# A hybrid recurrent decoder step on one core: the head of the program in another order

## The reference, cut to what matters

```python
def rmsnorm(x, g):
    y = x * lax.rsqrt(jnp.mean(x * x, axis=-1, keepdims=True) + EPS)
    return y * g
...
h = rmsnorm(x, g_mix[0])
z = h @ w_in_e[0]                       # 2048 -> 6 * 1024
xa, ga, q, fz, v, gb = jnp.split(z, EVEN_SPLIT_IDX, axis=-1)
...
lb = lb_logits ...                      # bound of the decay, per channel
logf = logaddexp(log(max(lb, 1e-30)), log1p(-lb) + log_sigmoid(fz))
k = (1 - lb) * sigmoid(-fz)
a = exp(-8 * sigmoid(r) * softplus(-lam_a))   # decay of the recurrence
...
x = x + mix;  x = x + conv_ffn(x)       # then a second layer, and a last rmsnorm
```

## Time and profile before

| | us |
|---|---|
| median of 3 runs | 2743.65 (2742.02 to 2745.71) |
| the profiled execution | 2744.42 |
| its span | 2742.7 |
| PE busy | 2699.8 (98%) |
| DVE busy | 1586.9 (58%) |
| ACT busy | 1176.5 (43%) |
| mean granted clock of PE | 0.993 |

### The profile page before, as it was taken

How to read it: one execution, slowest core, us unless ns; L and a number is a source line. 1 busy time by engine, 2 the same in 40 slices (tenths; PEclk the granted TensorE clock), 3 DMA queues, 4 the chain that set the end, 5 groups by cost and what they waited for, 6 DMA issues and landing times.

```text
span 2742.7 us, 54189 instructions
## 1 busy us (share of the span) xinstructions
PE 2699.8 (98%) x20003; PEld 2672.7 (97%) x20003; DVE 1586.9 (58%) x2605; ACT 1176.5 (43%) x1518; POOL 446.8 (16%) x533
## 2 busy tenths in 40 slices
PE   7999999999999999999999998999999999999998
PEld 7999999999999999999999996999999999999998
DVE  7556666665554455665556647565554555455554
ACT  5554455434343333435554343544433344333444
POOL 1333333330000000070003571310000000000023
PEclk9999999999999999999999999999999999999999
DMA  6444454555554545445454531555555555555543
GB/s 174 132 134 133 127 147 133 143 144 158 143 141 140 147 140 143 132 139 150 138 143 141 149 97 32 150 145 146 152 145 147 152 147 143 148 157 146 147 139 118
DMA packets 738479, 383.00 MB, mean 140 GB/s; under 512 B 13464, under 2 KB 734660, under 8 KB 738404
## 3 DMA queue, kind: packets, MB, share of 16 engines
q1 hardware_dynamic: 723088, 367.96, 47.1%
q0 software_dynamic: 2560, 7.29, 1.1%
q10 hardware_dynamic: 12756, 6.69, 0.8%
HBM read 373.31 MB, written 8.57 MB: 139 GB/s over the span
## 4 chain that ended last, share of the span: by engine, by line
PE 96%; DVE 3%; ACT 1%; issue 0%; DMA 0%; SPq 0%; DVEq 0%; ACTq 0%
PE banks L1629 31%; PE banks L1630 30%; PE banks L1631 30%; PE banks L1694 1%; PE banks L1909 0%; DMA xin<-in_x_sample 0%; DVE wl L1064 0%; DVE m L1506 0%; DVE m L1504 0%; PE banks L1690 0%; PE banks L2010 0%; PE banks L1792 0%; PE banks L1790 0%; DVE m L1505 0%; PE banks L1923 0%
## 5 line engine op out<-in xcount | busy, mean ns | idle before, releaser
L1064 DVE TENSOR_TENSOR wl<-raw,wh 128x1024 fp32r<-128x1024 f32 x708 | 899.3, 1271 | 802.1 <-ACT wh L496 801.1
L1629 PE MATMUL banks<-h,wh 128*128 128x336 f32 (+2 forms) x3648 | 1155.3, 317 | 3.9 <-DVE wl L1112 2.2
L496 ACT ACTIVATE wh<-raw 128x1024 fp32r<-128x1024 f32 x708 | 748.8, 1058 | 941.5 <-PE banks L1631 925.6
L1630 PE MATMUL banks<-h,wh 128*128 128x336 f32 (+2 forms) x3648 | 1146.2, 314 | 0.0
L1631 PE MATMUL banks<-h,wl 128*128 128x336 f32 (+2 forms) x3648 | 1144.9, 314 | 0.0
L1629 PEld LDWEIGHTS banks<-h,wh 128*128 128x128 f32 x3648 | 686.3, 188 | 11.7 <-issue 7.9
L1630 PEld LDWEIGHTS banks<-h,wh 128*128 128x128 f32 x3648 | 686.2, 188 | 1.7
L1631 PEld LDWEIGHTS banks<-h,wl 128*128 128x128 f32 x3648 | 685.9, 188 | 0.0
L1629 PE MATMUL banks<-act,wh 128*128 128x336 f32 (+2 forms) x1872 | 589.8, 315 | 2.6 <-DVE act L1580 2.0
L1630 PE MATMUL banks<-act,wh 128*128 128x336 f32 (+2 forms) x1872 | 586.5, 313 | 0.0
L1631 PE MATMUL banks<-act,wl 128*128 128x336 f32 (+2 forms) x1872 | 585.9, 313 | 0.0
(11 more groups left out here) (383 smaller groups left out, 1698.3 us busy)
## 6 DMA issues: line engine op xcount, KB each, us to landing
raw<-in_w_up SPq DMA_DIRECT2D x172, 512.0 KB, 4.0
raw<-in_w_gate SPq DMA_DIRECT2D x172, 512.0 KB, 3.9
raw<-in_w_down SPq DMA_DIRECT2D x160, 448.0 KB, 3.7
raw<-in_w_in_e SPq DMA_DIRECT2D x96, 512.0 KB, 3.8
raw<-in_w_out_e SPq DMA_DIRECT2D x32, 512.0 KB, 3.9
raw<-in_w_down SPq DMA_DIRECT2D x32, 512.0 KB, 3.9
raw<-in_w_in_c SPq DMA_DIRECT2D x16, 512.0 KB, 3.9
raw<-in_w_glu_v SPq DMA_DIRECT2D x16, 512.0 KB, 3.9
```

What stands on the lines that cost most here:

```text
L496: sc.activation(wh[:, j % RING, :], raw[:, j % RING, :], ACT.Copy).then_inc(rounded, 1)
L1064: v.tensor_tensor(wl[:, j % RING, :], raw[:, j % RING, :], wh[:, j % RING, :].bitcast(F32), ALU.subtract) \
L1629: pe.matmul(out, whi, hi, start=first and k == 0, stop=False)
L1630: pe.matmul(out, whi, lo, start=False, stop=False)
```

## The change

PE's queue begins with 28 matmuls of ones by ones (128 x 128, fp32) into a bank that nobody reads; the memset of ones is the DVE's first instruction. Then come the gains, chunks 0 to 11, and tile 0, with chunks 12 and 13 turned in its middle and 14 and 15 behind it. Tiles 0 and 1 wait for h_lo chunk by chunk (first_h) rather than once for all.

The transfers are reordered: column quarters 0 and 1, then weight tile 0, then row set 5 (which holds lam_a and lb), then quarters 2 and 3, then tiles 1 to 3 and the other rows. Two of the five parts of quarters 0 and 1 are issued by ACT's queue.

ACT's squares are three instructions of 2048 columns behind the chunk loop instead of twelve of 512 within it, and ACT copies seven of the chunks to X. DVE copies the rest, chunks 11 to 15 after the loop. Tile 0 is rounded and split after chunk 7, tile 1 after chunk 14. The reciprocal and the root are made of the sums (128 x 3) rather than of rs (128 x 336), so that the diagonal by ones gives rs at once, and DVE only copies it. That product (token_factors) and seven of the row sets now stand behind tile 3, and row set 5 behind tile 1. Row sets share banks side by side, so that PE needn't wait for ACT's copies, and ACT makes 3 copies of them instead of 7.

```diff
--- before.py
+++ after.py
+X_BY_ACT = (0, 1, 3, 4, 6, 7, 9)
+SPLIT_AFTER = (7, 14)
...
-        sqj, tsq, tss, DG = union(0, ("sqj", [P, 3, 4, D // 4]), ("tsq", [P, 3, 4]), ("tss", [P, 4]), ("DG", [P, 3, P]))
+        sqj, tsq, DG = union(0, ("sqj", [P, 3, D]), ("tsq", [P, 3]), ("DG", [P, 3, P]))
...
-        XB = (*bank[1:5], bank[6], bank[0])
-        RB = (bank[5], bank[3], bank[4], bank[6])
+        XB = bank[1:7]
+        row_sets = {0: (bank[0], 0, 80), 5: (BO, 0, 88), 1: (bank[4], 0, 86), 2: (bank[4], 86, 86), 3: (bank[5], 0, 86),
+                    4: (bank[5], 86, 86), 6: (bank[6], 0, 64), 7: (bank[6], 64, 96), 8: (bank[6], 160, 96)}
...
         @block.sync
         def _(e):
             e.dma_start(ident[:], a["c_ident"]).then_inc(consts_in, 16)
-            for g in (0, 2, 3):
-                x_columns(e, g)
+            for g in range(2):
+                x_columns(e, g, (2, 1, 3))
...
                 load(ph, 0, j, a["w_in_e"][0], 8 * (j % 2), 8, columns[j // 2])
+                if j == 0:
+                    load_rows(e, 5, head_rows_in)
+                    for g in range(2, 4):
+                        x_columns(e, g, range(5))
                 if j == RING - 1:
                     e.dma_start(masks[:], a["c_masks"]).then_inc(rows_in, 16)
...
+                    for q in (6, 7, 8, 1, 2, 3, 4):
+                        load_rows(e, q, rows_in)
...
-            x_columns(e, 1)
+            x_columns(e, 0, (4, 0))
+            load_rows(e, 0, gains_in)
+            x_columns(e, 1, (4, 0))
...
+            def token_squares(t):
+                n = (P, P, T - 2 * P)[t]
+                sc.activation(sqj[0:n, t, :], xin[0:n, t, :], ACT.Square, accum_out=tsq[0:n, t:t + 1]).then_inc(tok_sq, 1)
+
+            row_columns(1, (0,))
             e.wait_ge(rows_c, 1)
+            for c in range(DC):
+                e.wait_ge(x_t, c + 1)
+                if c in X_BY_ACT:
+                    sc.activation(X[:, c, :], XB[c % 6][:, 0:T], ACT.Copy)
+                sc.activation(h[:, c, 0, :], XB[c % 6][:, 0:T], ACT.Copy, scale=col("g_mix", c)).then_inc(h_hi, 1)
+                if c in SPLIT_AFTER:
+                    round_first(SPLIT_AFTER.index(c))
+            e.wait_ge(used, RING)
+            e.wait_ge(masks_made, 1)
             for g in range(4):
-                for c in range(4 * g, 4 * g + 4):
-                    e.wait_ge(x_t, c + 1)
-                    sc.activation(h[:, c, 0, :], XB[c % 6][:, 0:T], ACT.Copy, scale=col("g_mix", c)).then_inc(h_hi, 1)
-                if g >= 2:
-                    round_first(g - 2)
                 e.wait_ge(x_in[g], 80)
-                for t, n in enumerate((P, P, T - 2 * P)):
-                    ins = sc.activation(sqj[0:n, t, g, :], xin[0:n, t, g * (D // 4):(g + 1) * (D // 4)], ACT.Square,
-                                        accum_out=tsq[0:n, t, g:g + 1])
-                ins.then_inc(tok_sq, 1)
-            e.wait_ge(used, RING)
-            for j in (2, 3):
-                round_first(j)
-            norm_root(0)
-            for q in range(1, 9):
-                row_columns(q)
-            e.wait_ge(rows_c, 9)
+            round_first(2)
+            token_squares(0)
+            round_first(3)
+            token_squares(1)
+            token_squares(2)
+            row_columns(2, (5,))
+            e.wait_ge(ms_inv, 1)
+            sc.activation(tsq[:], tsq[:], ACT.Sqrt).then_inc(rstd, 1)
+            for turned, qs in ((4, (1, 2)), (6, (3, 4)), (9, (6, 7, 8))):
+                row_columns(turned, qs)
             e.wait_ge(lam_v, 1)
...
+            v.memset(ones[:], 1.0).then_inc(ones_made, 1)
             v.memset(tiny[:, 11, 0:1], 0.0).then_inc(split, CREDIT)
...
             for c in range(DC):
                 e.wait_ge(h_hi, c + 1)
-                v.tensor_copy(X[:, c, :], XB[c % 6][:, 0:T])
+                if c < 11 and c not in X_BY_ACT:
+                    keep(c)
...
-                if c in (11, 14):
-                    split_first((c - 11) // 3)
-            e.wait_ge(tok_sq, 4)
-            v.tensor_reduce(tss[:, 0:2], tsq[:, 0:2, :], mybir.AxisListType.X, ALU.add)
-            st.then(v.tensor_reduce(tss[0:80, 2:3], tsq[0:80, 2:3, :], mybir.AxisListType.X, ALU.add))
-            for t, n in enumerate((P, P, T - 2 * P)):
-                ins = v.tensor_scalar(DG[0:n, t, 0:n], ident[0:n, 0:n], tss[0:n, t:t + 1], None, ALU.mult)
-            ins.then_inc(diag_made, 1)
+                if c in SPLIT_AFTER:
+                    split_first(SPLIT_AFTER.index(c))
+            keep(12).then_inc(x_kept, 1)
+            split_first(2)
+            for c in (11, 13, 14, 15):
+                keep(c).then_inc(x_kept, 1)
+            split_first(3)
+            e.wait_ge(tok_sq, 3)
+            st.then(v.tensor_scalar(tsq[:], tsq[:], 1.0 / D, EPS, ALU.mult, ALU.add))
+            v.reciprocal(tsq[:], tsq[:]).then_inc(ms_inv, 1)
...
-            for j in (2, 3):
-                split_first(j)
-            norm_inverse(0)
-
+            e.wait_ge(rstd, 1)
+            for t, n in enumerate((P, P, T - 2 * P)):
+                ins = v.tensor_scalar(DG[0:n, t, 0:n], ident[0:n, 0:n], tsq[0:n, t:t + 1], None, ALU.mult)
+            ins.then_inc(diag_made, 1)
+            e.wait_ge(ms_done, 1)
+            st.then(v.tensor_copy(rs[:], BO[:, 0:T]))
...
-            e.wait_ge(rows_c, 9)
+            e.wait_ge(rows_c, 2)
...
+            e.wait_ge(ones_made, 1)
+            for k in range(28):
+                pe.matmul(BO[:, 0:P], ones[:], ones[:], start=True, stop=True)
+            e.wait_ge(consts_in, 16)
+            e.wait_ge(gains_in, 48)
+            rows_turned(0)
+            for c in range(12):
+                turned(c)
...
+                    if not ended and j == 2:
+                        e.wait_ge(x_kept, 1)
+                    half = None
                     if not ended and j == 0:
-                        e.wait_ge(h_lo, DC - 4)
-                    if not ended and j == 1:
-                        token_mean_squares()
-                        e.wait_ge(h_lo, DC)
-                    half = None
+                        half = lambda: (turned(12), turned(13))
+                    x = from_h if ended or j > 1 else first_h
...
+                    if not ended and j == 0:
+                        turned(14)
+                        turned(15)
                     if not ended and j == 1:
-                        e.wait_ge(rows_in, 16 * 16)
-                        for q in range(1, 9):
-                            if q >= 5:
-                                e.wait_ge(rows_c, q - 3)
+                        e.wait_ge(head_rows_in, 8 * 16)
+                        rows_turned(5)
+                    if not ended and j == 3:
+                        e.wait_ge(x_kept, 5)
+                        token_factors()
+                        e.wait_ge(rows_in, 8 * 16)
+                        for q in (1, 2, 3, 4, 6, 7, 8):
                             rows_turned(q)
```

More of the change, by code:

```diff
@@ L330, in build, with x_columns, load_rows @@
         ]
[L332 removed]
+        def x_columns(eng, g, parts):
             xp, xsm = a["x_prompt"][0], a["x_sample"].rearrange("s t d -> (s t) d")
             cols = slice(g * (D // 4), (g + 1) * (D // 4))
[L336 to L337 removed]
+            rows_of = ((0, 0, META, a["meta_tokens"]), (0, META, P, xp[0:P - META]), (1, 0, P, xp[P - META:2 * P - META]),
+                       (2, 0, META, xp[2 * P - META:SEQ]), (2, META, META + NS * LS, xsm))
+            for t, r0, r1, src in (rows_of[k] for k in parts):
                 eng.dma_start(xin[r0:r1, t, cols], src[:, cols]).then_inc(x_in[g], 16)
+        def load_rows(eng, q, arrived):
+            r = 0
+            for src, n in rowsets[q]:
+                eng.dma_start(rows[r:r + n, q, :], src).then_inc(arrived, 16)
+                r += n
         def one(t, c):
@@ L504, in norm_root, with row_columns @@
                 sc.activation(rs[:], rs[:], ACT.Sqrt).then_inc(rstd, 1)
[L506 to L509, removed]
-            x_columns(e, 1)
[L512 to L516, removed]
+            x_columns(e, 0, (4, 0))
+            load_rows(e, 0, gains_in)
+            x_columns(e, 1, (4, 0))
+            def row_columns(turned, qs):
+                b, n = row_sets[qs[0]][0], sum(row_sets[q][2] for q in qs)
+                c0 = (0, 80, 166, 252, 338, 424, 512, 576, 672)[qs[0]]
+                e.wait_ge(rows_t, turned)
+                sc.activation(prm[:, c0:c0 + n], b[:, 0:n], ACT.Copy).then_inc(rows_c, 1)
             def round_first(j):
@@ L1091, in _ @@
             v.memset(tiny[:, 11, 7:8], 0.0).then_inc(y_c, 2)
-            v.memset(ones[:], 1.0)
             v.memset(AT[:], 0.0)
+            v.memset(tsq[:], 1.0)
             e.wait_ge(consts_in, 16)
@@ L1658, in rows_turned, with turned @@
             def rows_turned(q):
-                w = (80, 86, 86, 86, 86, 88, 64, 96, 96)[q]
```

(8 more changed lines are left out.)

22 lines of the change are left out of this document (12 added, 10 removed).

## The result

| | before | changed |
|---|---|---|
| median of 22 runs each, us | 2743.94 (2741.04 to 2746.75) | 2748.64 (2745.81 to 2751.62) |
| ratio, 95% interval | | 1.0018 (1.0012 to 1.0024) |
| the profiled execution | 2744.42 | 2750.07 |
| its span | 2742.7 | 2748.4 |
| level 0 starts at | 47.19 | 53.04 |

The change costs 4.7 us. The forecast was 2749.8, 1.2 above the median, and + 6.2 at level 0, where + 5.85 was measured. The interval excludes "no change", though the difference lies under the 0.2% (5.5 us) that the prediction took as its bound. All of the profiled difference arises ahead of level 0, in these two executions.

The account below looks back on a forecast made before the run. PE is busy for 96%, but the stage was taken to end with the chain from the turned constants: 41.45 + 4.2 + 7.76 puts level 0 at 53.4, + 6.2 on 2743.65 gives 2749.8 us; range 2743.5 to 2753.5.

Parts of the forecast that it names:

- the chain from the turned constants: Through ACT's copies, DVE, Exp, split of tile 4, FZ and Q to level 0: 34.25 + 12.94 = 47.19 us before.
- Predicted end 10.45: PE's front: 28 products of ones end at 1.2 + 5.9 + 3.35 = 10.45 us; bounds 7.5 and 13.8.
- the sum's 5.9 us: PE's products of ones: dense work at half clock for 5.9 us before the clock rises, 13.1 products slow.
- The 14 copies: Chunk loop up to chunk 7: ACT's 14 copies at 0.42 each, 5.9 us; tile 0 starts at 19.35.
- the prediction's last sentence: Wrong if tile 4 follows at once, level 0 precedes 49, or PE waits for xin or raw in the head.
- just hidden: Quarter 2's last part, issued at about 12, lands by about 18 or 19, ahead of tile 0; at most 1 us otherwise.
- My 1.87 for the issue of tile 0: SP's queue ahead of quarter 2: issuing weight tile 0 takes 7.47 / 4 = 1.87 us, row set 5 some 3.5.
- the rival that had 0.17: It falls once more: clock drops in PE's 2.8 us idle ahead of tile 1; + 8 to + 9.2, 2752; chance 0.17.
- These three terms: Tile 1 at 29.6 to constants at 41.45, 4.2 to the split at 45.65, 7.76 to level 0 at 53.4.
- the side that had 0.46: Outcome "same", a difference within 0.2% (5.5 us): chance 0.46; slower 0.49, faster 0.05.
- The clock stays up: PE rises early in the products and doesn't fall in the loop, tile 0 fast: + 2.1, 2745.8 us; chance 0.22.
- The head start is kept: Tile 4's weights ready when constants are turned: level 0 at 45.9, 1.3 ahead, up to 6.9 us faster; chance 0.08.

Follow-up runs that it names:

- both edits: Changed kernel with row set 5, the Exp and DVE's operations on the constants ahead of tile 1, and seven row sets turned behind tile 1: 1.0006 of before.
- the factors early: On top of both edits: product by ones behind tile 2, rs copied behind the splits of tiles 4 and 5, squares spread: 2740.46 us, 0.9989 of before.
- without products: Changed kernel without the 28 products of ones at its front: 2749.05 us, 1.0017 of before.
- the clock kept up: Changed kernel with further products of ones, 2 behind each of chunks 5 to 10 and 8 behind chunk 11: 2751.12 us, 1.0027 of before.
- the constants early: Changed kernel with row set 5 turned ahead of tile 0, its copy, the Exp and DVE's operations on the constants behind chunk 11: 2746.28 us, 1.0006 of before.
- all three with the factors early: The kernel with the factors early with 28, 12 or no products of ones: 0.9989, 0.9989 and 0.9986 of before.
- the two single edits: Changed kernel with only the seven row sets turned behind tile 1 (1.0014 of before), or only the constants' operations early (1.0006).

## Why the prediction was right

**Where the time goes.** The prediction's central step was that the stage ends with the chain from the turned constants, and that the change moves its start. The chain in the trace is that one. The run with both edits, in which two of its entrances are open, and the one with the factors early, in which it is gone, show it as the cause: level 0 went from 53.04 to 49.90 to 45.13, and the ratio from 1.0018 to 1.0006 to 0.9989. From level 0 to the end the profiled executions of all kernels took 2693.2 to 2698.1, without order, so nothing of the loss is seen to come later, within this scatter of 5 us.

**The products.** Predicted end 10.45, gains turned at 10.37. They take 0.43 us each and then 0.22, where the prediction had 0.45 and 0.225 from the product by ones in the earlier trace rows, and which of the two from the transposes. The Trainium skill, "TensorE: Matmul & The Clock Gate", Part 1 on the clock gate, has the clock throttled by default and released by activity: the rate agrees, the column of the granted clock (1.00 from the start) doesn't. But the moment of the rise isn't fixed. Over the eight profiled executions with 28 products it came 3.4 to 5.9 us after the first of them, and they ended between 9.15 and 10.4; the changed kernel's is the latest of the eight. That the sum's 5.9 us and 10.45 were met so closely is luck.

**The chunk loop and quarter 2.** The 14 copies took from 11.00 to 16.51, so 0.39 each where I had 0.42, and tile 0 started at 19.03, not 19.35. Quarter 2 did bind PE's transposes of chunks 8 to 11, for 1.78 us. By the prediction's last sentence a wait of PE for xin is a sign that it is wrong, so on this point it was. As a cover for tile 0, which it had called just hidden, it held: ACT rounded tile 0 from 16.51 on while PE turned these chunks, and tile 0 came no later. The chain of waits leads through this transfer all the same (9.79 to 15.67, then the transposes and 1.92 of "issue"), so the cover was nearly used up. My 1.87 for the issue of tile 0 was wrong; I had divided a group by its count, and row set 5 took 3.1 where I had 3.5. The last part of quarter 2 was issued at 9.79, not at 12, and landed at 15.67, not at 18 or 19. The timeline of SP's queue in the changed kernel:

```profile
4.20 0.68 SPq L449 DMA_DIRECT2D raw<-in_w_in_e  x1
...
13.09 4.56 SPq L449 DMA_DIRECT2D raw<-in_w_in_e  x3
```

**Tiles 0 and 1.** Half clock for tile 0's first 5.2 us where I had taken 5.9; with its transposes 6.77 where I had 6.95. PE's gap ahead of tile 1 was 2.54 by the record, where I had 2.8. Tile 1 at 29.09 (29.6 predicted), at full clock. Ten of the profiled kernels have this same gap, and in six of them the clock fell in it or within the first 1.3 us of tile 1: without products, with the clock kept up, with the constants early and in all three with the factors early. In the other four, the changed kernel among them, it stayed up. So the rival that had 0.17 was closer than I gave it, and that tile 1 ran fast in the changed kernel is in part luck; what decides it stays open.

**From tile 1 to level 0.** 11.90 to the constants (11.85 predicted), 4.30 from there to the split (4.2), 7.75 to level 0 (7.76). These three terms carried the result. The first and the last are prices of the kernel before; the 4.2 is its 5.18 less what the row sets' new banks and the earlier table load save, and that held too (1.42 from the transposes to the table load for 1.35, then 1.63 and 1.25 as before). The prediction didn't see that DVE's copy of rs was a second way into the same chain, only 0.3 us behind; it cost this sum nothing.

**The size.** 53.04 for 53.4, the difference all from the chunk loop and tile 0. The profiled execution had + 5.65, the medians have + 4.7: one execution lies up to 3 us from its median here, so the sum was right for the execution and a little high for the median. The late end of the products in this execution may be a part of that; the others of the changed kernel weren't profiled. **The chances.** The measured + 4.7 lies below the bound of 5.5, on the side that had 0.46; slower by more than that had 0.49. The ratio's interval reaches from + 3.3 to + 6.6 us and so straddles the bound, so the run doesn't decide between the two.

**The rivals.** "The clock stays up" would have given + 2.1, with tile 0 at full clock: the trace has half. "The head start is kept" named the right place, the wait ahead of tile 4, and was right that it decides; it became true only when the Exp, the row copies and the factors no longer stood ahead of that split.

## What to carry to other kernels

An earlier start of the bound engine is worth nothing if a chain through other engines decides the end of the stage; follow that chain first, and ask of each moved piece which link of it now starts later. When such a chain has several entrances (here the Exp, the row copies and the copy of the factors in queues that run in order), open all of them before judging one: the two single edits gave 0.7 and 1.9 us, both together 2.7, and with the factors level 0 came 7.9 us earlier than in the changed kernel, for only then did PE no longer wait. Idle time that appears on the bound engine ahead of such a chain is its shadow; filling it changed nothing here.

## What the runs showed of the hardware

- The granted clock reads 1.00 ahead of its first recorded change, while the starts of the products' records lay 0.213 us apart and from 7.12 us on 0.112. Twelve transposes took 2.35 us with the column at 0.52, and 24 took 4.69 with the column at 1.00. Rates tell what the column doesn't.
- The rise came at different moments in the same work, 3.4 to 5.9 us after the first of 28 products, which ended between 9.15 and 10.4 us. A gain of 1 us in the head can't be read from one profile.
- Half clock is not quite twice the time: matmuls of 336 columns started every 0.28 us instead of 0.153, and products of ones took 0.43 instead of 0.22.
- The clock could fall in a pause of 2.2 to 2.5 us: after 12 products, the last of them at the fast rate, and 2.2 us without work it read 0.52; in a pause of 2.54 us behind tile 0, or just behind it, it fell in six kernels of ten (0.82, then 0.50 in the one with more products), but not in the changed kernel.
- The table load took 1.28 us, and the Exp behind it started 0.01 us later (42.41 to 43.70).
- ACT's square of 2048 columns took 1.90 us to the next instruction (29.04 to 30.94), where four of 512 columns had cost 4 x 0.53.
